# The loads, scatters, forget rows and last products of a two-layer decoder step, in another order

## The reference

```python
def pool_mixer(u, prev, pos0, w_grp, scale):
    # sums over the last 2, 4, 8, 16 rows, by group of columns
    diff = (pooled - u...).astype(u.dtype)
    out = einsum('ntgc,gcd->ntgd', diff, w_grp).reshape(n, t, D_MODEL)
    return out * scale, ext[:, -POOL_STATE:]

def hier_moe(x, norm_g, w_rg, w_re, w_gate, w_up, w_down):
    u = rms_norm(x, norm_g)
    # top group of 4, top 2 of its 4 experts -> dense_w
    h = silu(einsum('ntd,edf->ntef', u, w_gate)) * einsum('ntd,edf->ntef', u, w_up)
    h = h * dense_w[..., None]
    return einsum('ntef,efd->ntd', h, w_down)

c_all = cumsum(concatenate([logf_past, logf_s], axis=1), axis=1)   # forget sums over the cache
```

## Time and profile before

| | us |
|---|---|
| three runs | 1480.87, 1483.19, 1484.49; median 1483.19 |
| span of the profiled execution | 1482.9 |
| TensorE busy | 1346.8 (91%) |
| VectorE, ScalarE, GpSimd busy | 518.5, 309.1, 173.7 |
| transfers | 437.15 MB, mean 295 GB/s |
| first mixture | about 101 to 407 |
| second mixture | about 1157 to 1476 |

### The profile page before, as it was taken

One profiled execution on the slowest core, in us unless ns is written; L12 is line 12 of the kernel. 1 busy time (PEld: TensorE's weight loads), 2 busy tenths in 40 slices (PEclk: granted clock), 3 DMA queues, 4 the chain that ended last, 5 costly groups with the idle time before them and its releaser, 6 DMA issues.

```text
span 1482.9 us, 37368 instructions
## 1 busy us (share of the span) xinstructions
PE 1346.8 (91%) x15938; PEld 1027.1 (69%) x15938; DVE 518.5 (35%) x1163; ACT 309.1 (21%) x728; POOL 173.7 (12%) x206
## 2 busy tenths in 40 slices
PE   5998999999887889998989899989996799999996
PEld 5888888888535666766665556556445788888883
DVE  3351110000175546464646766663024200000005
ACT  2130100000142221313133443434011000010110
POOL 1012000000302000111111111210000300000002
PEclk9899999999988999999999998997997899999998
DMA  9269999999996679797978997974263589999985
GB/s 307 84 249 307 383 392 393 390 388 388 367 362 225 221 247 358 257 370 267 334 241 274 295 308 240 331 256 158 95 269 135 153 302 384 388 385 385 385 331 187
DMA packets 147690, 437.15 MB, mean 295 GB/s; under 512 B 21319, under 2 KB 51912, under 8 KB 138607
## 3 DMA queue, kind: packets, MB, share of 16 engines
q1 hardware_dynamic: 99319, 367.64, 67.7%
q10 hardware_dynamic: 37296, 38.09, 7.6%
q0 software_dynamic: 10960, 29.80, 6.7%
HBM read 406.38 MB, written 29.45 MB: 294 GB/s over the span
## 4 chain that ended last, share of the span: by engine, by line
PE 47%; DMA 24%; issue 13%; DVE 7%; ACT 4%; SPq 3%; ACTq 1%; POOL 1%; POOLq 0%; DVEq 0%
DMA W<-in_w_up 18%; PE PS L1276 9%; PE PS L1411 5%; PE PS L1039 4%; PE PS L1072 3%; PE PS L1067 3%; PE PS L1035 3%; PE PS L1317 2%; PE PS L976 2%; PE PS L1355 2%; PE PS L1375 2%; PE PS L1363 2%; PE PS L968 1%; DMA out_k_prompt<-W 1%; DMA W<-in_cache_v 1%
## 5 line engine op out<-in xcount | busy, mean ns | idle before, releaser
L1035 PE MATMUL PS<-W,KV 128*32 128x384 f32 x3072 | 343.4, 488 | 15.3 <-DMA W<-in_w_up 10.6
L1039 PE MATMUL PS<-W,KV 128*32 128x128 f32 x3072 | 346.4, 274 | 0.0
L1039 PEld LDWEIGHTS PS<-W,KV 128*32 128x32 f32 x3072 | 334.2, 110 | 1.4
L2119 DVE TENSOR_TENSOR KV<-KV,PS 128x384 f32<-128x384 f32 x32 | 17.7, 554 | 479.6 <-PE PS L1053 443.6
L1276 PE MATMUL PS<-W 128*128 128x256 f32 x768 | 181.1, 390 | 0.7 <-ACT KV L1681 0.7
L1276 PEld LDWEIGHTS PS<-W 128*128 128x128 f32 x768 | 146.5, 196 | 32.4 <-issue 10.4
L1067 PE MATMUL PS<-W,KV 128*32 128x384 f32 x1440 | 163.9, 493 | 3.5 <-ACT KV L1587 3.5
L1072 PE MATMUL PS<-W,KV 128*32 128x256 f32 x960 | 163.9, 329 | 0.0
L1035 PEld LDWEIGHTS PS<-W,KV 128*32 128x32 f32 x3072 | 141.0, 110 | 22.7 <-DMA W<-in_w_up 16.5
L2260 DVE STREAM_TRANSPOSE KV<-KV 128x1024 f32<-128x1024 f32 x128 | 154.8, 1225 | 0.0
L1072 PEld LDWEIGHTS PS<-W,KV 128*32 128x32 f32 x960 | 96.0, 110 | 15.1 <-issue 0.2
(11 more groups left out here) (293 smaller groups left out, 1581.0 us busy)
## 6 DMA issues: line engine op xcount, KB each, us to landing
W<-in_w_gate SPq DMA_DIRECT2D x32, 2048.0 KB
W<-in_w_up SPq DMA_DIRECT2D x32, 2048.0 KB, 22.0
W<-in_w_down SPq DMA_DIRECT2D x32, 2048.0 KB, 11.5
KV<-in_cache_k SPq DMA_DIRECT2D x256, 256.0 KB, 5.3
W<-in_cache_v SPq DMA_DIRECT2D x128, 512.0 KB, 7.9
yd<-KV ACTq DMA_DIRECT2D x30, 288.0 KB, 7.0
W<-in_w_kvf SPq DMA_DIRECT2D x4, 2048.0 KB, 25.8
W<-in_w_kvf ACTq DMA_DIRECT2D x8, 1024.0 KB, 8.3
```

The source lines that it names most:

```text
L1035: pe.matmul(PS[32 * q:32 * q + 32, bank, 0:WIDE], x, w[:, k, 0:WIDE], start=(k == 0), stop=(k == KC - 1), tile_position=(0, 32 * q), skip_ ...
L1039: mm = pe.matmul(PS[CAP:P, bank, P * q:P * q + P], x, w[:, k, WIDE:FF], start=(k == 0 and q == 0), stop=(k == KC - 1), tile_position=(0, C ...
```

## The change

What is computed stays the same. The edits:

- Start: the band matrix of tile 0 (512 of 2304 columns) is loaded by itself, the others behind tile 1, and both the norm and the sums of tile 1 wait for them. VectorE waits for `png` and the bands only before the multiplication that needs `png`. ScalarE takes one square root of a zero first, so that its table is loaded before the data come. `pool_weights` runs ahead of the first copy of sums.
- First mixture, SyncE's queue: gate(0), up(0), down(0) and gate(1) are issued together at the end of the start's loads; down(1) when part 0 of the forget sums is read, up(1) when all are; then a quarter of the forget rows, gate(2) and up(2), three quarters, down(2), gate(3), up(3), the rows of ones (`qtd`), down(3), the pool states, and the loop from expert 4.
- Places: TensorE makes 12 of 16 heads, the ranks, the last 4 heads, the lists, and then parts 1 and 2, in PSUM banks 4 and 5 rather than 2 and 3. The first `x_tr` no longer waits for ScalarE's last copy; the first `h_tr` does.
- Both mixtures, GpSimd: the ten scatters of row numbers (used only if an expert has more than 96 rows) come after all gathers of experts' rows rather than after two.
- Both mixtures, TensorE: the product gate(15) comes ahead of down(14).
- Second mixture, VectorE: the hidden rows of expert 15 come ahead of the first `combine`.

```diff
-            sp.dma_start(bands, A["bands"]).then_inc(sem("pool_in"), 16)
+            first = BAND["cur"][0]
+            sp.dma_start(bands[:, 0:first], A["bands"][:, 0:first]).then_inc(sem("pool_in"), 16)
             sp.dma_start(psc, A["pool_scale"][0:1, :].to_broadcast([P, D])).then_inc(sem("pool_w_in"), 16)
             sp.dma_start(pw, A["pool_w"].rearrange("a g (c p) n -> p (a g) c n", p=P)).then_inc(sem("pool_w_in"), 16)
             sp.dma_start(H[:, 1, :], A["x_prompt"][0, P - META:2 * P - META, :]).then_inc(sem("tile_in_1"), 16)
+            sp.dma_start(bands[:, first:], A["bands"][:, first:]).then_inc(sem("tile_in_1"), 16)
...
+                def rest(start):
+                    with sp.Fori(start, NE - 1, 2) as e:
                         for j in range(2):
                             for which in range(3):
                                 load(e + j, which, j)
-                return first, second, rest, load
...
-            first, second, rest, _ = moe_weights(0)
-            first(0)
-
-            sp.wait_ge(sem("un_ready"), NT)
-            first(1)
+            rest, load = moe_weights(0)
+            for which in range(3):
+                load(0, which, 0)
+            load(1, 0, 1)
+
+            sp.wait_ge(sem("forget_pe"), NH // 2)
+            load(1, 2, 1)
+            sp.wait_ge(sem("forget_pe"), NH // 2 + 4)
+            load(1, 1, 1)
+
+            def forget_out(part):
+
+                hs = slice(NH // 4 * part, NH // 4 * part + NH // 4)
+                sp.dma_start(RPD[hs].rearrange("h g r -> g h r"), RQ[:, hs, :]).then_inc(sem("rq_out"), 16)
 
             sp.wait_ge(sem("forget_ready"), NH // 2 + 4)
-            second()
-            sp.dma_start(RPD.rearrange("h g r -> g h r"), RQ).then_inc(sem("rq_out"), 16)
+            forget_out(0)
+            load(2, 0, 0)
+            load(2, 1, 0)
+            for part in range(1, 4):
+                forget_out(part)
+
+            load(2, 2, 0)
+            load(3, 0, 1)
+            load(3, 1, 1)
 
             for j in range(NT):
                 lo, n = CONST["ones"][0], min(P, TP - j * P)
                 sp.dma_start(QTD[:, DH, j * P:j * P + n], C[0:NH, lo:lo + n]).then_inc(sem("rq_out"), 16)
+
+            load(3, 2, 1)
...
-            rest()
+            rest(4)
...
-            second()
+            load(1, 1, 1)
+            load(1, 2, 1)
...
+                with pool.Fori(2, NE - 1, 2) as e:
+                    for j in range(2):
+                        gather(e + j, j)
+
                 pool.wait_ge(sem("routed"), 4 + l * 4)
                 for ch in range(2):
                     for t in range(NT):
                         r = ROWS[t]
                         pool.indirect_dma_start(out=LIST[l], out_offset=bass.IndirectOffsetOnAxis(ap=SSi[0:r, ch, t:t + 1], axis=0),
                                                 in_=ids[0:r, t:t + 1], in_offset=None).then_inc(sem("scattered"), 16)
-                with pool.Fori(2, NE - 1, 2) as e:
...
-                    for h in range(NH):
+                    for h in heads:
                         if h >= 4 and h % 2 == 0:
                             pe.wait_ge(sem("forget_ready"), h // 2 - 1)
...
                         for h in range(4 * n, 4 * n + 4):
-                            out = PS[:, 2 + n % 2, (h % 4) * P:(h % 4) * P + P]
+                            out = PS[:, 4 + n % 2, (h % 4) * P:(h % 4) * P + P]
...
             def places(l):
 
                 if l == 0:
-                    forget_sums(0)
+                    forget_sums(0, range(0, 12))
...
                 if l == 0:
-                    forget_sums(1)
+                    forget_sums(0, range(12, NH))
...
                 mm.then_inc(sem("ranks"), 1)
                 if l == 0:
+                    forget_sums(1)
                     forget_sums(2)
-
-                    pe.wait_ge(sem("forget_ready"), NH // 2 + 4)
...
                         pe.wait_ge(sem("onto_step"), 3 + l * 3)
+                        pe.wait_ge(sem("forget_ready"), NH // 2 + 4)
...
-                def expert(e, j, last=False):
+                def halves(e, j, which):
+
                     count = 8 * e + 16 - 8 * j
+                    if which == 0:
+                        pe.wait_ge(sem("xt_ready"), e + 1 + l * NE)
+                        after(pe, sem("silu_done"), e + l * NE)
+                        product(2, 3 * j, count, "gate")
+                    else:
+                        product(3, 3 * j + 1, count, "up")
+
+                def expert(e, j):
                     first = isinstance(e, int) and e == 0
-                    pe.wait_ge(sem("xt_ready"), e + 1 + l * NE)
-                    after(pe, sem("silu_done"), e + l * NE)
-                    product(2, 3 * j, count, "gate")
-                    product(3, 3 * j + 1, count, "up")
-                    if last:
-                        return
+                    halves(e, j, 0)
+                    halves(e, j, 1)
...
                 h_tr(NE - 2)
+                halves(NE - 1, 1, 0)
                 down(NE - 2, 0)
-                expert(NE - 1, 1, last=True)
+                halves(NE - 1, 1, 1)
                 h_tr(NE - 1)
...
-                        pe.wait_ge(sem("pool_in"), 32)
+                    if t < 2:
+                        pe.wait_ge(sem("tile_in_1" if t else "pool_in"), 32)
...
-                act.wait_ge(sem(f"tile_in_{t}"), (32, 16, 16, 16, 48)[t])
+                act.wait_ge(sem(f"tile_in_{t}"), (32, 32, 16, 16, 48)[t])
...
+            act.wait_ge(sem("zeros"), 2)
+            act.activation(sd[:, 0:1], V4[:, 0:1], ACT.Sqrt)
             pool_norm(0)
...
+                if gain_in is not None:
+                    dve.wait_ge(sem(gain_in[0]), gain_in[1])
...
                     pool_rows(t + 1)
+                if t == 0:
+                    pool_weights()
                 if t < NT:
...
                 if t == 0:
-                    pool_weights()
...
                 npass = dve.value_load(npi[0:1, 0:1], min_val=1, max_val=PASSES)
-                if l == 1:
-                    combine(1, 0)
                 hidden(NE - 1)
                 if l == 1:
-                    for n in range(1, NT):
+                    for n in range(NT):
                         combine(1, n)
                 with dve.If(npass > 1):
                     with dve.Fori(1, npass) as p:
```

More of the change, by code:

```diff
@@ L566, in load @@
                         sp.dma_start(w_slot(3 * j + which, which), w_src_dyn(l, e, which)).then_inc(sem(f"w_in_{3 * j + which}"), 16)
-                def first(part):
-                    if part == 0:
-                        load(0, 0, 0)
-                        load(0, 1, 0)
-                    else:
-                        load(0, 2, 0)
-                        load(1, 0, 1)
-                def second():
-                    load(1, 1, 1)
-                    load(1, 2, 1)
-                def rest():
-                    with sp.Fori(2, NE - 1, 2) as e:
+                def rest(start):
+                    with sp.Fori(start, NE - 1, 2) as e:
                         for j in range(2):
@@ L813, in moe @@
                                                 in_=ids[0:r, t:t + 1], in_offset=None).then_inc(sem("scattered"), 16)
-                with pool.Fori(2, NE - 1, 2) as e:
-                    for j in range(2):
-                        gather(e + j, j)
                 if l == 1:
@@ L1922, in then, with norm @@
                 dve.wait_ge(sem("dve_step"), steps[0])
-            def norm(phase, t, out, gain=None):
+            def norm(phase, t, out, gain=None, gain_in=None):
                 r, n = ROWS[t], NORMS.index((phase, t))
```

16 lines of the change are left out of this document (7 added, 9 removed).

## The result

The changed kernel takes 1490.22 us (median of 20 runs, 1483.37 to 1499.31), the kernel before 1483.78 in the same comparison (20 runs, 1474.34 to 1493.93). The ratio is 1.0047, 95% interval 1.0026 to 1.0068: slower by 0.5%, against a forecast of 1476.2.

What follows compares the result with a forecast made beforehand. TensorE (busy 91% of the span) and the DMA engines were taken to be both at their limit in a mixture. Terms -1.8, 0, -3.3, +1.5, -2.2 and -1.2 summed to -7.0, giving 1476.2 us, range 1473 to 1479.

Steps and rivals of the forecast that it cites:

- Scatters: Both mixtures: late scatters cost nothing; in the second, TensorE's wait for the gather of expert 2 goes, -2.2 us.
- steps past 18.5 us while the scatters run: Sign, in the mixtures' steps per expert, that would show the forecast wrong.
- Rival (3): Near both mixtures' ends, late scatters hold the transfers up: 7.5 us a mixture, 1491.2 us in all; chance 0.08.
- the two weights alone explain a slow gather: Reason against Rival (3): two weights ahead of expert 2's gather account for its 11.8 us, against 4.35 for the first.
- The other reason: Reason against Rival (3): the step of 17.62 us that follows the first mixture's scatters is not long.
- Weights of the first mixture: First mixture's first two steps: earlier loads remove the stalls for gate(2) and up(2), 39.00 to 35.68, -3.3 us.
- Start: Kernel's start: split bands and earlier pool_weights bring tile 1's mixer products to 27.2 from 28.98, -1.8 us.
- The estimate by which a fixed cost of the split load would leave nothing of it: Start: about 2.0 us fixed per DMA could make its gain about nothing instead of -1.8.
- Places: Lists and forget rows before the first transposes: same matmuls end at the same time, 0, bounds -2.5 to +1.8 us.
- End of the first mixture: gate(15) ahead of down(14) delays the store to yd: +1.5 us, between 0 and +3.6.
- End of the kernel: Last combine starts 3.6 us later, but additions no longer wait for TensorE: -1.2 us, bounds 0 and -3.7.
- Rival (1): First mixture: transfers stay ahead, steps run at TensorE's 17.6 us, up to 6.0 us more gain, 1470.2; chance 0.14.

Runs made afterwards that it cites:

- e2: Kernel before with only the ten scatters moved behind the loop of gathers in both mixtures; 1489.91 us, ratio 1.0051.
- e5: Changed kernel with the ten scatters in the middle, behind the gathers of experts 0 to 3; 1477.54 us, ratio 0.9967 to the kernel before.
- e12: Kernel before with the change's start alone (split bands, table of roots first, VectorE's new order); 1479.24 us, ratio 0.9989.
- e1: Changed kernel with the ten scatters back ahead of the loop of gathers; 1486.14 us, ratio 1.0015 to the kernel before.
- e3: Changed kernel without the scatters and the waits for them; 1480.76 us, ratio 0.9979 to the kernel before.
- e4: Changed kernel with five scatters back ahead of the loop of gathers and five behind it; 1483.37 us, ratio 1.0009 to the kernel before.
- e8: Changed kernel with ten plain stores at the late place instead of the indirect scatters; 1492.28 us, ratio 1.0069 to the kernel before.
- e10: Changed kernel with scatters behind the gathers of experts 0 to 3 and down(14) ahead of gate(15) again; 1471.94 us, ratio 0.9929 to the kernel before.
- e11: Changed kernel with the ten scatters halfway through both mixtures, behind the gather of expert 7; 1484.56 us, ratio 1.0003 to the kernel before.
- e7: Changed kernel with scatters behind the gathers of experts 0 to 3, TensorE's last products and VectorE's first combine in old order; 1474.67 us, ratio 0.9943.
- e9: Changed kernel with the ten late scatters turned into reads of 4 bytes a partition; 1477.77 us, ratio 0.9968 to the kernel before.
- e6: Kernel before with only the ten scatters moved to the middle, behind the gathers of experts 0 to 3; 1480.35 us, ratio 0.9981.

## Why the prediction was wrong, step by step

**The step that failed** is under Scatters: "At their new place, behind the last gather, GpSimd has nothing to do until the results." I asked who waits for GpSimd and found nobody; the cost is on the transfers. The new place cost 7.7 us in the first mixture and 4.9 in the second, 12.6 against a forecast of nothing; the sign named for it, steps past 18.5 us while the scatters run, came. Rival (3) had the mechanism, at a chance of 0.08. That it also had the size, 7.5 a mixture and 1491.2 for the time (median 1490.2), is luck. It took 7.5 as the difference between a gather behind two weights and one on idle engines, 11.8 and 4.35. Issue to landing of such a gather in the kernel before, first in 1158 to 1178 us (behind the scatters), then in 155 to 173 us (no scatters, the transfers full):

```profile
KV<-xs,idc POOLq DMA_INDIRECT x1, 11.8
```
```profile
KV<-xs,idc POOLq DMA_INDIRECT x1, 10.0
```

The eleven in 1200 to 1400 us have a median of 10.3. So full transfers alone make it 10.0 to 10.3, and some 1.5 to 1.8 of the 7.5 are left for the scatters. My reason against the rival, "the two weights alone explain a slow gather", was right as far as it went; it only said nothing on what the scatters do to weights. The other reason was a misreading: the step of 17.62 in the earlier trace rows does follow the scatters, but it is the one after the one that they hit: that is 21.38.

**Weights of the first mixture, -3.3.** The two steps took 17.62 + 17.72 = 35.3 us, forecast 35.7, but my reason was wrong. I put the stalls of the earlier trace rows on the stores that delayed gate(2). In e2 those stores and the old order of loads are unchanged and only the scatters are gone. Timeline of SyncE's queue there:

```profile
102.74 16.96 SPq L620 DMA_DIRECT2D qtd<-C  x5
...
123.49 0.39 SPq L566 DMA_DIRECT2D W<-in_w_gate  x1
...
134.45 0.39 SPq L566 DMA_DIRECT2D W<-in_w_down  x1
...
152.06 0.38 SPq L566 DMA_DIRECT2D W<-in_w_down  x1
```

gate(2) goes out 1.5 us later than before, and still the step is 17.61. Its down(5) goes out at 188.43, the changed kernel's at 188.30. What the new order of loads does is to open the hole in which e5 hides the scatters; by itself it was worth nothing here. So a gain was booked on the loads that belonged to the scatters, and with it went the sign that they were dear.

**Start, -1.8.** Measured -1.4 to -1.6 (27.57, and 27.41 in e12, instead of 28.98). Right. The estimate by which a fixed cost of the split load would leave nothing of it did not come true.

**Places, 0, bounds -2.5 to +1.8.** The first transposes stood at 101.04, and at 99.44 with the start alone: +1.6. In the kernels with this part of the change they came at 100.8 to 101.5 seven times (after, e1, e3, e4, e8, e10, e11) and at 99.6 to 99.8 three times (e5, e7, e9), so it is between 0 and +2. What sets the two groups apart stays open.

**Scatters, second mixture, -2.2.** From the first gather to the first down 40.6 instead of 41.9 after, 39.8 in e2: -1.2 and -2.0. Right in kind.

**End of the first mixture, +1.5.** The profiles of after and before differ by +1.2, of which 1.1 is the first gather from `yd` (19.8 against 18.7 us behind the last load). Over all kernels with the new order this gather comes 1.7 to 2.9 us later than in e2, e6 and e12, where down(14) ran at the full clock after its wait, and -0.6 to +1.2 later than in before, e7 and e10, where it did not. That is about what the bounds of 0 and +3.6 held; where in them it falls hangs on a clock that the sum did not have.

**End of the kernel, -1.2.** Measured -0.8. The two parts were also seen rightly: 3.6 us given up (4.0 measured), and 4.8 won on VectorE (44.2 to 39.4), which is what the forecast's 3.6 + 1.2 makes.

**Rival (1)**, the head start that lasts, did not come: the steps of the first mixture were back at 18.2 by 206 us. With the terms as measured the sum is -3.0 for the start up to down(5), +8.6 for the rest of the first mixture, +1.2, -1.2, +4.1, -0.8: +8.9 on what the change touches; the medians differ by 6.4. The forecast's sum with 12.6 in place of nothing would be -7.0 + 12.6 = +5.6, close to the medians and to the +5.2 of the spans. That too is in part luck: the spans are so near only because the attention was 4.0 shorter in one profile than in the other.

## What to carry to other kernels

Where DMA engines and TensorE are both full, ask of every small store not who issues it but which large loads are in flight meanwhile: 1152 numbers of 4 bytes, on a queue that took 4.5% of the engines' time with its gather, cost 5 to 8 us a time. Put them into a hole of the transfers and look for it in GB/s by stretch, not in the engines' share. And before a stall is put on one of two candidates that stand side by side in a trace, price the other one too: the stall that I read as slow issue was the very cost that the change then moved to a worse place.

## What the runs showed that I had not expected

- Small writes slow the packets of other queues (10.62 MB instead of 12.34 in 35 us at the same share of engine time); small reads, as many and as large, do not. The slow stretch outlasts the last scatter's issue (342.65) by some 6 us: 121 GB/s from 346 to 349.
- Plain stores are no cheaper than indirect ones, but take GpSimd less time to issue: 5.43 us for ten instead of 12.4.
- A stall near the middle of a mixture is partly made good: eight steps of 17.6 us follow it in the first mixture of e11, where there are 18.0 to 18.5 elsewhere.
- A pause of 3.4 to 7 us of TensorE is followed by rows at the lower clock (0.86 us instead of 0.52). The long steps of after, e2, e8 and e11 are 1.5 to 3.1 us longer than 17.61 and the pause together, which I put down to it. At the mixtures' ends a pause of 1.7 us is followed by the lower clock in some runs and not in others.
